# Three first pieces split a stage earlier, a final sum made by halves, the gate product with its inputs in the outer loop, expert biases split beside the logits

## What is computed

```python
# layer 1, the end of the state-space mixer
z = gelu(y);  z = z * sigmoid(z @ w_glu);  mix = z @ ssm_w_out
# layer 2, the end of the attention
mix = heads @ att_w_out
# third block: merge of the two attentions, and the residual
merged = sigmoid(ga) * (ya @ w_oa) + sigmoid(gb) * (yb @ w_ob)
x = x + g_a * (merged @ w_out)
# experts: logits, the four best, a softmax over them, the experts' rows, their weighted sum
logits = h @ router_w + router_b;  top_logit, top_e = top_k(logits, 4);  top_w = softmax(top_logit)
act = (up + 1) * (gate * sigmoid(1.702 * gate))          # up and gate clipped, with biases b_up, b_gate
y = act @ w_down[e] + b_down[e]
x = x + g_m * sum_over_4(y * top_w)
```

## Time and profile before

| | |
|---|---|
| median of 3 runs | 3155.54 us (3152.6 to 3156.43) |
| the profiled execution | 3153.39 us, of which the span is 3151.6 us |
| busy in that span | PE 93%, PE weight load 74%, DVE 65%, ACT 50%, POOL 14% |
| mean granted TensorE clock | 0.963 of full speed |

### The profile page before, as it was taken

One profiled execution on the slowest core, in us unless ns is written; L12 is line 12 of the kernel. 1 busy time (PEld: TensorE's weight loads), 2 busy tenths in 40 slices (PEclk: granted clock), 3 DMA queues, 4 the chain that ended last, 5 costly groups with the idle time before them and its releaser, 6 DMA issues. The chain is left out here.

```text
span 3151.6 us, 41825 instructions
## 1 busy us (share of the span) xinstructions
PE 2942.7 (93%) x15092; PEld 2340.1 (74%) x15092; DVE 2051.6 (65%) x2429; ACT 1581.3 (50%) x1694; POOL 445.0 (14%) x405
## 2 busy tenths in 40 slices
PE   7979999997899999899998869999999999999995
PEld 3658788764688888776677758888888888888882
DVE  8442223658642235745753389999999999999993
ACT  5232322324532223434532257777777777777771
POOL 1001200021212100003100011111221112111211
PEclk8889999997999999999999879999999999999997
DMA  5512222202022322110012459999999999999983
GB/s 232 225 68 81 103 98 107 84 36 74 15 107 81 120 82 112 40 63 20 1 57 104 162 209 386 389 386 378 380 386 393 381 381 386 386 388 377 385 338 142
DMA packets 86285, 641.54 MB, mean 204 GB/s; under 512 B 9728, under 2 KB 10176, under 8 KB 22880
## 3 DMA queue, kind: packets, MB, share of 16 engines
q1 hardware_dynamic: 75568, 601.60, 49.4%
q0 software_dynamic: 10224, 37.23, 3.0%
q10 hardware_dynamic: 384, 1.19, 0.1%
HBM read 616.36 MB, written 23.63 MB: 203 GB/s over the span
## 5 line engine op out<-in xcount | busy, mean ns | idle before, releaser
L2889 DVE TENSOR_TENSOR arena_rounded<-arena,arena_rounded 128x2048 fp32r<-128x2048 f32 x420 | 951.3, 2286 | 94.5 <-ACT arena_rounded L2885 94.5
L2885 ACT ACTIVATE arena_rounded<-arena 128x2048 fp32r<-128x2048 f32 x420 | 801.8, 1919 | 212.2 <-PE banks L263 139.9
L261 PE MATMUL banks<-arena_rounded,operand_rounded 128*128 128x512 f32 (+1 forms) x2064 | 820.7, 398 | 11.3 <-DVE operand_rounded L546 7.9
L262 PE MATMUL banks<-arena_rounded,operand_rounded 128*128 128x512 f32 (+1 forms) x2064 | 804.2, 390 | 0.0
L263 PE MATMUL banks<-arena_rounded,operand_rounded 128*128 128x512 f32 (+1 forms) x1504 | 585.1, 389 | 0.0
L261 PEld LDWEIGHTS banks<-arena_rounded,operand_rounded 128*128 128x128 f32 x2064 | 390.5, 189 | 90.2 <-DVE operand_rounded L546 8.3
L262 PEld LDWEIGHTS banks<-arena_rounded,operand_rounded 128*128 128x128 f32 x2064 | 390.6, 189 | 78.5 <-issue 1.2
L263 PEld LDWEIGHTS banks<-arena_rounded,operand_rounded 128*128 128x128 f32 x1504 | 284.7, 189 | 59.2
L261 PE MATMUL banks<-operand_rounded,arena_rounded 128*128 128x512 f32 (+2 forms) x712 | 267.2, 375 | 6.0 <-PE banks L263 5.2
L262 PE MATMUL banks<-arena_rounded,arena_rounded 128*128 128x512 f32 (+1 forms) x688 | 267.7, 389 | 0.0
L263 PE MATMUL banks<-operand_rounded,arena_rounded 128*128 128x512 f32 (+2 forms) x712 | 263.7, 370 | 0.0
(11 more groups left out here) (469 smaller groups left out, 3860.9 us busy)
## 6 DMA issues: line engine op xcount, KB each, us to landing
arena<-in_gate SPq DMA_DIRECT2D x140, 1024.0 KB, 6.7
arena<-in_up SPq DMA_DIRECT2D x140, 1024.0 KB, 7.1
arena<-in_down SPq DMA_DIRECT2D x140, 1024.0 KB, 6.4
arena<-in_dense SPq DMA_DIRECT2D x62, 2048.0 KB, 7.9
arena<-routed SPq DMA_DIRECT2D x4, 2048.0 KB, 14.5
arena<-in_dense SPq DMA_DIRECT2D x6, 1024.0 KB, 5.2
small<-in_rows SPq DMA_DIRECT2D x7, 512.0 KB, 8.0
resid<-in_x SPq DMA_DIRECT2D x4, 512.0 KB, 7.0
```

Of the source, the lines that this page charges most:

```text
L261: nc.tensor.matmul(out, left[0], right[0], start=start, stop=False)
L262: nc.tensor.matmul(out, left[0], right[1], start=False, stop=False)
L2885: nc.scalar.activation(high[q % NHI], raw[:, q, :], ACT.Copy).then_inc(high_ready, 1)
L2889: nc.vector.tensor_tensor(low[q], raw[:, q, :], high[q % NHI].bitcast(F32), ALU.subtract).then_inc(low_ready, 1)
```

## The change

Six edits. (1) The first piece of "ssm_out" is split in `ssm_gate`. (2) The first piece of "att_out" is split in `attention_heads`, its weights in four quarters of 128x512. (3) The first piece of "blend_out" is split in `blend_merge`. The stages behind them start their first matmuls without a wait (`prepared`). (4) The gate product's loops are exchanged: input tile outside, output tile inside, so that it can start at the first gelu. (5) The expert biases are loaded by SP in `norm_turned`, ahead of the expert pieces, and split in `route` while PE makes the logits. (6) `combine` works by halves of 128x512, PE makes all bias products first, and DVE adds to the residual two halves later.

```diff
 project_residual
-            for m in range(pieces):
+            for m in range(1, pieces):
                 k.split_high(act, chunk0, m, used, high)
 projection
+    prepared, fed = (3, None) if fed == "prepared" else (0, fed)
-            if t == 0:
-                pe.wait_ge(low, 3 * (m + 1))
+            if t == 0 and 3 * (m + 1) > prepared:
+                pe.wait_ge(low, 3 * (m + 1) - prepared)
 ssm_gate, DVE
+                if n == 0:
+                    dve.wait_ge(out_high, 1)
+                    k.split_low(first, 0, out_low)
+                if n >= 2:
+                    dve.wait_ge(out_high, n)
+                    nc.vector.tensor_tensor(left[:, 1, n - 2, :], gated[:, n - 2, :], left[:, 0, n - 2, :].bitcast(F32),
+                                            ALU.subtract).then_inc(out_low, 1)
 ssm_gate, ACT
+            k.split_high(act, first, 0, None, out_high)
             for n in range(WT):
                 act.wait_ge(product, n + 1)
                 nc.scalar.activation(gate[:, n, :], k.psum[:, n, :], ACT.Sigmoid).then_inc(opened, 1)
+                if n in (1, 2):
+                    act.wait_ge(made, n)
+                    nc.scalar.activation(left[:, 0, n - 1, :], gated[:, n - 1, :], ACT.Copy).then_inc(out_high, 1)
 ssm_gate, PE
-            pe.wait_ge(gelu, WT)
-            for n in range(WT):
-                for c in range(WT):
+            for c in range(WT):
+                pe.wait_ge(gelu, c + 1)
+                for n in range(WT):
 attention_heads, DVE (loop over n; N is 32)
+                if 21 <= n < 25:
+                    dve.wait_ge(out_high, n - 20)
+                    V.tensor_tensor(out_in_place[:, quarter(n - 21)], out_raw[:, quarter(n - 21)],
+                                    out_rounded[:, quarter(n - 21)].bitcast(F32), ALU.subtract).then_inc(out_low, 1)
+                if n >= N + 2:
+                    f = n - N - 2
+                    dve.wait_ge(left_high, f + 1)
+                    V.tensor_tensor(left[:, 1, f, :], a["out"][:, f, :], left[:, 0, f, :].bitcast(F32),
+                                    ALU.subtract).then_inc(out_low, 1)
 attention_heads, ACT
+                if 19 <= n < 23:
+                    nc.scalar.activation(out_rounded[:, quarter(n - 19)], out_raw[:, quarter(n - 19)],
+                                         ACT.Copy).then_inc(out_high, 1)
+                if n >= N:
+                    f = n - N
+                    act.wait_ge(kept, ST * NH // 2 - NH // 2 + f + 1)
+                    nc.scalar.activation(left[:, 0, f, :], a["out"][:, f, :], ACT.Copy).then_inc(left_high, 1)
 blend_merge, ACT, behind its last sigmoid
+            k.split_high(act, FIRST["w_out"], 0, None, out_high)
+            act.wait_ge(used, M - 1)
+            act.wait_ge(added, 2)
+            for f in range(2):
+                nc.scalar.activation(k.left[:, 0, 0, f, :], merged[:, f, :], ACT.Copy).then_inc(out_high, 1)
 blend_merge, DVE, ahead of the last four L2561
+                if m == M - 1:
+                    dve.wait_ge(out_high, 1)
+                    k.split_low(FIRST["w_out"], 0, out_low)
+                    for f in range(2):
+                        dve.wait_ge(out_high, f + 2)
+                        V.tensor_tensor(k.left[:, 0, 1, f, :], merged[:, f, :], k.left[:, 0, 0, f, :].bitcast(F32),
+                                        ALU.subtract).then_inc(out_low, 1)
 load_route
+    for n in range(2):
+        sp.dma_start(e["bias_raw"][n * NE:(n + 1) * NE, :], k.io["moe_bias"]).then_inc(inputs, 16)
-    sp.wait_ge(inputs, 32)
+    sp.wait_ge(inputs, 64)
 route, ACT (first instead of last) and DVE (before the wait for the logits instead of ahead of L2831)
+            act.wait_ge(bias_zero, 2)
+            nc.scalar.activation(e["bias"], e["bias_raw"], ACT.Copy).then_inc(bias_split, 1)
+            dve.wait_ge(bias_split, 1)
+            V.tensor_tensor(e["bias"][low, :], e["bias_raw"][low, :], e["bias"][low, :].bitcast(F32), ALU.subtract)
 combine, PE
+            pe.wait_ge(biases_in, 16)
+            for u, (t, c) in enumerate(units):
+                nc.tensor.matmul(k.psum[:, u, :], e["spread_t"][:, t * P:(t + 1) * P], b_down[:, half(c)], start=True, stop=False)
+            pe.wait_ge(diagonals, 2 * ST)
+            for u, (t, c) in enumerate(units):
+                if c == 0:
+                    pe.wait_ge(rows_in[t], 16)
+                for n in range(2):
+                    i = nc.tensor.matmul(k.psum[:, u, :], diag[:, 2 * t + n, :], rows[:, t, n, half(c)],
+                                         start=False, stop=(n == 1))
 combine, DVE (POOL and SP go by the same 8 halves)
+            for u in range(N + LAG):
+                if u < N:
+                    t, c = units[u]
+                    dve.wait_ge(product, u + 1)
+                    if u >= 4:
+                        dve.wait_ge(gated, u - 3)
+                    V.scalar_tensor_tensor(out=acc[:, u % 4], in0=rows[:, t, 2, half(c)], scalar=w(t, 2), in1=k.psum[:, u, :],
+                                           op0=ALU.mult, op1=ALU.add).then_inc(partial, 1)
+                    dve.wait_ge(partial, u + 1)
+                    V.scalar_tensor_tensor(out=acc[:, u % 4], in0=rows[:, t, 3, half(c)], scalar=w(t, 3), in1=acc[:, u % 4],
+                                           op0=ALU.mult, op1=ALU.add).then_inc(summed, 1)
+                if u >= LAG:
+                    t, c = units[u - LAG]
+                    dve.wait_ge(gated, u - LAG + 1)
+                    V.tensor_tensor(k.resid[:, t, half(c)], rows[:, t, 0, half(c)], k.resid[:, t, half(c)], ALU.add).then_inc(added, 1)
```

More of the change, by code:

```diff
@@ L540, in _ @@
             V = nc.vector
-            for m in range(pieces):
-                dve.wait_ge(high, 3 * m + 1)
+            for m in range(1, pieces):
+                dve.wait_ge(high, 3 * m - 2)
                 k.split_low(chunk0, m, low)
                 for j in range(2):
-                    dve.wait_ge(high, 3 * m + j + 2)
+                    dve.wait_ge(high, 3 * m + j - 1)
                     V.tensor_tensor(k.left[:, m % 2, 1, j, :], lhs(2 * m + j), k.left[:, m % 2, 0, j, :].bitcast(F32),
@@ L694, in scalar @@
     def scalar(act):
-        if fed is None:
+        if fed is None and not prepared:
             ahead(act)
@@ L753, in vector @@
         V = nc.vector
-        for m in range(M):
+        for m in range(1 if prepared else 0, M):
             raw, w_low, w_high, left = parts_of(m)
@@ L1361, in ssm_gate @@
     summed, gelu, product, opened, rows_turned, rows_kept, rows_out = (k.sem(f"gate_{n}") for n in names)
-    mod_rows = k.work[0:8 * DT, 16384:16384 + P]
-    g0 = FIRST["ssm_glu"]
+    mod_rows = k.work[0:8 * DT, 19456:19456 + P]
+    g0, first = FIRST["ssm_glu"], FIRST["ssm_out"]
+    made, out_high, out_low = (k.sem(f"gate_{n}") for n in ("made", "out_high", "out_low"))
+    left = k.arena_r[8][:, 0:PIECE].rearrange("p (h k s) -> p h k s", h=2, k=2)
     with nc.Block() as block:
@@ L1823, in attention_heads @@
     score, masked, exped, inverse, scaled, turned, placed_even, placed_odd, product, kept = (k.sem(f"heads_{n}") for n in names)
+    first = FIRST["att_out"]
+    out_high, out_low, left_high = (k.sem(f"heads_out_{n}") for n in ("high", "low", "left"))
+    out_raw, out_in_place, out_rounded = k.piece(first, 0)
+    quarter = lambda n: slice(n * NB, (n + 1) * NB)
+    left = k.arena_r[8][:, 0:PIECE].rearrange("p (h k s) -> p h k s", h=2, k=2)
     def at(x, n, e):
@@ L2419, in blend_merge @@
      added) = (k.sem(f"merge_{n}") for n in names)
+    out_high, out_low = (k.sem(f"first_out_{n}") for n in ("high", "low"))
     sub = k.stat[:, 0:1]
@@ L2696, in _ @@
                                      ACT.Copy).then_inc(copied, 1)
-            act.wait_ge(bias_in, 32)
-            act.wait_ge(bias_zero, 2)
-            nc.scalar.activation(e["bias"], e["bias_raw"], ACT.Copy).then_inc(bias_split, 1)
         @block.tensor
@@ L3087, in combine @@
     nc = k.nc
+    units = [(t, c) for t in range(ST) for c in range(2)]
+    N, LAG = len(units), 2
     rows = k.arena[:, 0:ST * NK * D].rearrange("p (t n d) -> p t n d", t=ST, n=NK)
     diag = k.turned_flat[:, 0:2 * ST * P].rearrange("p (n s) -> p n s", n=2 * ST)
-    acc = k.turned_flat[:, 2 * D:4 * D].rearrange("p (n d) -> p n d", n=2)
+    acc = k.turned_flat[:, 2 * D:4 * D].rearrange("p (n d) -> p n d", n=4)
     b_down = k.turned_flat[0:NE, 4 * D:5 * D]
-    g_m = k.gate_rows[:, D:2 * D]
     names = ("diagonals", "product", "partial", "summed", "gated", "added")
@@ L3096, in combine @@
     rows_in = [k.sem(f"combine_rows_in_{t}") for t in range(ST)]
-    def add_tile(V, dve, t):
-        dve.wait_ge(gated, t + 1)
-        V.tensor_tensor(k.resid[:, t, :], rows[:, t, 0, :], k.resid[:, t, :], ALU.add).then_inc(added, 1)
+    half = lambda c: slice(c * NB, (c + 1) * NB)
     with nc.Block() as block:
@@ L3108, in _ @@
                 sp.dma_start(rows[:, t], src[t]).then_inc(rows_in[t], 16)
```

(32 more changed lines are left out.)

45 lines of the change are left out of this document (15 added, 30 removed).

## The result

The changed kernel takes 3130.24 us (median of 4 runs, 3128.97 to 3134.49), the kernel before 3154.07 in the same group (3150.4 to 3156.43). The ratio is 0.9929, with a 95% interval of 0.9916 to 0.9942: 22.4 us less, between 18.3 and 26.5. Two further groups of runs gave 0.9947 (0.9932 to 0.9963) and 0.9929 (0.9915 to 0.9943). The forecast was 3129 us and 25.4 us less. The profiled execution took 3134.49 us (span 3132.6), the slowest of its four, so one trace is not enough to judge a term of one us. From here on I use stage lengths of all 14 executions that were profiled: three of the changed kernel, ten of its variants and a single one of the kernel before, whose lengths so have no spread.

What follows compares the result with a forecast made beforehand. PE, busy 93% of the span, was taken as the bound, with its idle time at stage starts and serial tails to gain. 4.2 + 6.3 + 5.5 + 1.2 + 0.6 + 7.6 = 25.4 us less gave 3129 us, range 3121 to 3138.

Steps and rivals of the forecast that it cites:

- ssm_out: Start of this stage: PE begins at 194.4 instead of 198.65, a gain of 4.2 us, with no gain of clock counted.
- att_out: Start of this stage: PE begins 4.85 us earlier, less 0.4 in the heads, plus 1.8 of clock: gain 6.3 us.
- The 0.4 for growing units: In the attention heads, DVE's quarter split is slightly too long, so four units grow by 0.1 us each.
- blend_out: Start of this stage: PE begins 5.5 us earlier; the clock brings 0 to 2.4 us more, taken as 1.2.
- Biases: Expert biases loaded and split earlier: 1.2 us gained at the end of `route`, 0.6 lost on SP, net gain 0.6.
- cost 0 to 1.2, taken 0.6: End of `norm_turned`: two more DMAs in SP's full queue make SP end between 1787.8 and 1789.5, costing 0.6 us.
- combine: Last stage: work by halves with all bias products first ends at 3144.0, a gain of 7.6 us, bounds 5.5 and 10.4.
- at the warm pace of the diagonal ones they take 0.48 each: In the last stage, 16 bias records at 0.48 us each, at most 0.56, take 7.7 to 9 us.
- rival (a): The clock stays low in the last stage and falls in the "blend_out" gap: 22 us gained, 3132 us; chance 0.17.
- (c): PE finds another wait at the stages' starts, so about 15 of the 25 us go: 3145 us; chance 0.07.
- (d): Slower: loads become the pace of the experts' 35 rounds, 3180 us at 1.5 us each; chance 0.03.
- (b): Moved splits lengthen `ssm_gate` and the heads' units, SP holds the router's stage: 18 us gained, 3136 us; chance 0.14.

Runs made afterwards that it cites:

- biases_last: The changed kernel, but in `combine` each half's bias product comes behind its four diagonal records: 3131.1 us, ratio 0.9939 to the kernel before, `combine` 43.4 us.

## Why the prediction was right, and where it was not

The time was right (3130.2 for 3129, inside 3121 to 3138). By its own steps it was right in part:

- **"ssm_out"**: right. The gap is 4.38 us (4.5), and PE starts 20.8 us after the first gelu where I had 21.6. The gate product itself took 16.40 us in the kernel before and 15.4 to 15.7 in nine of the changed kernels, which the forecast had unchanged. In the four traces of the last group the clock rose later under it (16.8 to 17.0 us), and the gain was 3.6 to 3.8 instead of 5.0 to 5.3. With the product at its 16.40 every one of the 13 traces gives 4.2 or 4.3, for my 4.2; the rest of this term is the clock.
- **"att_out"**: right in the start (4.9 for 4.85) and in the clock: PE was 10.2 us ahead at its first product and 12.1 once had risen too, 1.9 for my 1.8. The 0.4 for growing units was wrong: with the wait moved the heads take the 92.3 us of before. I missed the wait that I had passed over as free: 1.0 us, a table load behind it.
- **"blend_out"**: right in the start (5.5). For the clock I took the middle of 0 and 2.4; it held in ten of thirteen executions, which is the upper bound, and fell in three, behind the same gap of 2.4 us. Those three show that the gap alone does not decide it; what does stays open.
- **Biases**: wrong in sign. The step that failed is "cost 0 to 1.2, taken 0.6" for SP's queue (measured 1.5 in the mean, up to 1.8; SP's list grew by 3.1 us, from 9.98 to 13.08, where its steps of 0.9 and about 1.3 make 2.2), and one that was not there: PE came out of the longer gap with less time at 2.4 GHz, and the logits cost 1.4 more. The 1.2 at the end of `route` was right. The Trainium skill's rule that I weighed there (DMA: Bandwidth & Descriptors, Rules for kernel authors) pointed the right way, against the edit; whether the 32 partitions were the reason no run here tells.
- **`combine`**: wrong by 6.1 of 7.6 us (1.5 found in the mean, 1.3 in the trace of the changed kernel, to which the rest of this point refers). The failed step is "at the warm pace of the diagonal ones they take 0.48 each". I took the 1.12 us of a pair in the earlier trace rows as a sign that 32 rows don't matter to the clock, but those pairs ran between full ones, after the clock had risen. Behind the gap all sixteen ran at 0.85 each, which puts the first sum 5.1 us late (rival (a) had the mechanism and priced it at 2.1). The other 1.2 are the halves: 18.7 us from the first sum to the end of POOL's last product, where I had 17.5. The 2.28 per half matched my 2.3 only by luck: I had POOL as the pace, but it waits 0.63 us per half. The rule of the Trainium skill (GPSIMD Engine Reference, Specifications), contention between POOL and DVE instructions with two SBUF inputs, holds in the trace: POOL takes 1.65 us instead of 1.27. What I left out is the other side, which sets the pace here: DVE is slowed as well, 0.98 instead of 0.75.

The found terms add up to 3.6 to 5.3, then 5.8 ("att_out" with the heads and the clock), 8.0 ("blend_out"), -1.8 and 1.5: 17.1 to 18.8 us, and 1.6 to 2.4 less where the clock fell at "blend_out". From the profiled 3153.39 that gives 3134.6 to 3136.3 us, inside the range of 3121 to 3138 but outside the narrower 3125.5 to 3131.5 of the forecast. The two misses are 8.5 us (6.1 and 2.4), against which 1.3 us of clock at "blend_out" and up to 1.1 in `ssm_gate` came in more than forecast.

The two profiled executions differ by 19.0 us of span. By the same stretches 16.5 of it lie where the edits work and 2.5 where no edit does, 1.6 of these ahead of `ssm_gate`: 170.9 us in the trace of before, the longest of 14 (164.8 to 170.0 in the others). I have no cause for that. The 22.4 us are a difference of medians; their interval (18.3 to 26.5) overlaps the found terms, and the second group had 16.7, so the record does not show where the last 4 us come from, or that they are there. That 3130.2 fell so close to 3129 is luck: two terms were wrong, and the executions lay some us in my favour.

Rivals (c) and (d) did not occur: PE waits on nothing else at the three starts, and `experts` kept its 1273.0 (1272.0 to 1273.7), so the pieces of the first round were in time. (The sum in (d) is off a little: 35 rounds of 0.9 us less 25.4 are 6.1 us, just under 0.2%.) Of (b), the moved blocks fitted beside the work; only the stage of the router was held up.

## What to carry to other kernels

A piece that is split in the stage in front pays what the timeline says, as soon as the other engines have idle time there; all three starts came within 0.12 us of the forecast gap. Look at what the move puts in front of other things: a wait at the head of an engine's list can hold up a table load, and two more DMAs ahead of twelve of 1 MB held up the end of a stage by 1.5 us in the mean, and PE's clock with it. Don't put all low products (few rows) first behind a long gap: filling their operands up to 128 rows with zeros took `combine` from about 43 to 36 us, four halves ahead and four behind to 38.4. Doing the full ones first, with each bias product behind them, brought nothing (43.4).

## What the hardware showed that I had not expected

- After a gap of 18.3 to 18.7 us, 16 records of 32x512 kept the granted clock at 0.50 for all of their 14.0 us, in all seven traces that had them (14.01 or 14.02 us), and it rose 2.7 to 5.5 us after the start of the first record of 128 rows behind them; with 128 rows (identity and residual in one kernel, padding with zeros in the other) the clock rose 4.6 and 5.3 us after their start and they took 9.4 and 9.7 us.
- The same sequence of products (four records of 128 rows, two of 32) behind a gap of 24.5 to 24.8 us saw the clock rise 2.9 to 3.4 us after its start in three executions and only after 8.7 in a fourth (`biases_last`); and behind a gap of 2.4 us it held in ten and fell in three.
- A DVE scalar-tensor-tensor of 128x512 with two SBUF inputs took 0.98 us beside a POOL multiplication and 0.75 without; the one with an input in PSUM kept 0.73 to 0.75. POOL's took 1.65 beside DVE and 1.27 mostly alone.
